# Hyena's transforms by residues of time modulo four, in a one-core encoder layer

## The reference

```python
h = rms_norm(x, norm_mix)
u_hy, q, k, v = split(h @ w_in, [1536, 2048, 2176])

def hyena_filter_spectra(...):                  # a sine network, 2 orders, forward and backward
    filt = (a @ w3).reshape(L, 2, 2, 512) * exp(-t * deltas)
    k2 = concatenate([fwd, 0, reversed bwd])    # 1024 rows of time
    return rfft(k2 / (sum(abs(k2), axis=0) + EPS), axis=0)

def hyena_mixer(u, short_w, short_b, skip, k_f):
    u = depthwise convolution of u over time, 3 taps, + short_b
    v, g1, g2 = split(u, 3)
    z = v
    for o, gate in enumerate((g1, g2)):
        z = gate * (irfft(rfft(z, n=1024) * k_f[o], n=1024)[:512] + skip[o] * z)
    return z

y = concat(group_rms_norm(y_hyena, 8 groups), group_rms_norm(y_attention, 8 heads))
x = x + y @ w_out
```

## Time and profile before

| what | value |
|---|---|
| runs, device us | 796.03, 793.9, 798.8; median 796.03 |
| span of the profiled execution | 791.7 us |
| instructions in it | 10886 |
| HBM read and written | 141.81 MB, 12.58 MB |
| mean DMA rate over the span | 195 GB/s |

### The profile page before, as it was taken

How to read it: one execution, slowest core, us unless ns; L and a number is a source line. 1 busy time by engine, 2 the same in 40 slices (tenths; PEclk the granted TensorE clock), 3 DMA queues, 4 the chain that set the end, 5 groups by cost and what they waited for, 6 DMA issues and landing times.

```text
span 791.7 us, 10886 instructions
## 1 busy us (share of the span) xinstructions
PE 747.9 (94%) x3680; PEld 607.8 (77%) x3680; DVE 603.7 (76%) x930; ACT 461.6 (58%) x689; POOL 78.0 (10%) x94
## 2 busy tenths in 40 slices
PE   5899999999999898889999999999999999999994
PEld 3664858788898787678787787888888888888882
DVE  5767482997799877835548568899899999999882
ACT  5952333131233988621559333787888888887782
POOL 0000000000000000000000001122222232222111
PEclk9999999999999999999999998999999999999997
DMA  8830203020120200022130675999999999999741
GB/s 291 298 107 1 84 23 106 27 80 1 38 96 27 78 31 1 2 62 97 54 116 18 246 294 182 420 364 385 379 372 383 373 391 372 369 369 383 306 159 21
DMA packets 28542, 146.53 MB, mean 185 GB/s; under 512 B 4791, under 2 KB 6711, under 8 KB 21976
## 3 DMA queue, kind: packets, MB, share of 16 engines
q1 hardware_dynamic: 23320, 135.53, 45.3%
q0 software_dynamic: 5184, 10.50, 5.0%
HBM read 141.81 MB, written 12.58 MB: 195 GB/s over the span
## 4 chain that ended last, share of the span: by engine, by line
PE 72%; DVE 15%; ACT 6%; DMA 4%; issue 3%; SPq 0%; POOL 0%; DVEq 0%; ACTq 0%; POOLq 0%
PE bank L1992 17%; PE bank L2378 11%; PE bank L2380 10%; PE bank L2379 10%; PE bank L1930 9%; PE bank L1937 3%; DMA slot<-in_w_down 2%; PE bank L2373 2%; PE bank L2004 1%; ACT w_hi L727 1%; PE bank L2292 1%; PE bank L2290 1%; PE bank L2291 1%; DVE w_lo L1165 1%; PE bank L2415 1%
## 5 line engine op out<-in xcount | busy, mean ns | idle before, releaser
L1849 DVE TENSOR_TENSOR e_lo<-slot,e_hi 128x1024 fp32r<-128x1024 f32 x192 | 221.4, 1218 | 9.4 <-ACT e_hi L1045 9.3
L1045 ACT ACTIVATE e_hi<-slot 128x1024 fp32r<-128x1024 f32 x192 | 188.2, 1061 | 7.7 <-DMA slot<-in_w_down 4.9
L1165 DVE TENSOR_TENSOR w_lo<-w_raw,w_hi 128x1024 fp32r<-128x1024 f32 x41 | 49.4, 1222 | 69.8 <-ACT w_hi L727 69.6
L727 ACT ACTIVATE w_hi<-w_raw 128x1024 fp32r<-128x1024 f32 x41 | 42.7, 1057 | 96.9 <-DMA w_raw<-in_w_in 63.2
L2378 PE MATMUL bank<-e_hi,hgT_hi 128*128 128x512 f32 x240 | 95.0, 396 | 0.3 <-DVE hgT_lo L1861 0.3
L2380 PE MATMUL bank<-e_hi,hgT_lo 128*128 128x512 f32 x240 | 93.6, 390 | 0.0
L2379 PE MATMUL bank<-e_lo,hgT_hi 128*128 128x512 f32 x240 | 93.4, 389 | 0.0
L2378 PEld LDWEIGHTS bank<-e_hi,hgT_hi 128*128 128x128 f32 x240 | 45.2, 189 | 9.5 <-DVE hgT_lo L1861 0.7
L2380 PEld LDWEIGHTS bank<-e_hi,hgT_lo 128*128 128x128 f32 x240 | 45.1, 188 | 9.6
L2379 PEld LDWEIGHTS bank<-e_lo,hgT_hi 128*128 128x128 f32 x240 | 45.1, 188 | 8.9
L2378 PE MATMUL bank<-e_hi,gaT_hi 128*128 128x512 f32 x120 | 48.1, 401 | 0.0
(11 more groups left out here) (395 smaller groups left out, 1671.6 us busy)
## 6 DMA issues: line engine op xcount, KB each, us to landing
slot<-in_w_down SPq DMA_DIRECT2D x16, 2048.0 KB, 16.6
slot<-in_w_gate SPq DMA_DIRECT2D x16, 2048.0 KB, 14.6
slot<-in_w_up SPq DMA_DIRECT2D x16, 2048.0 KB, 16.0
w_raw<-in_w_in SPq DMA_DIRECT2D x18, 512.0 KB, 3.5
w_raw<-in_w_out SPq DMA_DIRECT2D x8, 512.0 KB, 3.7
w_raw<-in_w_k_mem SPq DMA_DIRECT2D x4, 512.0 KB, 6.1
x_in<-in_x SPq DMA_DIRECT2D x4, 512.0 KB, 9.2
w_raw<-in_w_v_mem SPq DMA_DIRECT2D x4, 512.0 KB, 6.0
```

The lines of the kernel that those rows point to most:

```text
L727: act.activation(w_hi[ring(m)][:], w_raw[ring(m)][:], ACT.Copy).then_inc(s_wh, 1)
L1045: act.activation(e_hi[buffer(b, j)][:], slot[slot_][:, 1024 * part:1024 * (part + 1)], ACT.Copy).then_inc(s_ehi, 1)
L1165: dve.tensor_tensor(w_lo[slot_][:], w_raw[slot_][:], w_hi[slot_][:].bitcast(F32), ALU.subtract)\
L1849: dve.tensor_tensor(e_lo[slot_][:, at_], slot[slot_][:, at_], e_hi[buffer(b, j)][:].bitcast(F32), ALU.subtract)\
```

## The change

The convolutions are split by the residue r of time modulo four (`NR`) and the channels into two halves h of 256 (`HC`), where before it was parity and halves of the frequencies.

- **Forward and spectra.** A job is one residue, its cosine part in the left half of a bank and its sine part in the right: six fp32r products of 256 columns for z, fp32 products of 256 columns for the filter. DVE puts the residues together in two levels (`butterfly`, `second_sums`; `spec_sums` for the filter, whose residues 1 and 3 PE sums itself with a negated copy `dft_neg`).
- **Products.** `spectrum` and `filtered` take the place of `pointwise`: instructions of 2048 and 1024 elements.
- **Inverse and gates.** `inv_jobs` has `idft` as the stationary operand, so the results have time on partitions and need no transposes. The gates are turned instead (`gate_jobs`, copied out by ACT's `gate_rows`), and `gated` multiplies inverse and gate. `z_half_hi` and `z_half_lo` split order 1's input.
- **Norm and skip.** `gate_taps` puts the filter's norm into the gate's taps and bias; `skip_added` adds skip x norm to the filter's first row, for which `l1_row` sums the norm as a row. `skip_row` is a new load of 1024 values of 4 bytes.
- **Banks.** Jobs of this stage have fixed banks (`STAGE_BANKS`); filters use four.
- **Order.** g1, q, kv, g2 are the weights' order; forward, inverse and gates stand between single pieces of them; the constant products of this stage go. `roped` has the gains multiplied into its tables once (`rope_gains`) and ACT squares the keys. `outer_taps` takes two instructions of 511 for each block, not four of 255 or 256.
- **In the attention** the norm's sums are DVE reductions over the free axis; the rows of Hyena are multiplied by the inverse, turned (`hyena_rows`), and split as they leave PSUM (`hyena_rows_hi` on ACT, `hyena_rows_lo` on DVE).

```diff
+STAGE_BANKS = {"filt": lambda o, t, way: (2 * t + way) % 4, "mv": lambda j: 4 + j, "l1row": lambda o: 7, "l1": lambda o: 6 + o,
+               "spec": lambda o, h, r: 4 + SPEC_ORDER.index(r), "fwd": lambda o, h, r: 4 + R_ORDER.index(r),
+               "u": lambda c: c % 4, "q": lambda i: i, "kv": lambda i: i, "zT": lambda r: r,
+               "gT": lambda o, r: 6 + r % 2, "inv": lambda o, h, rp: 4 + 2 * h + rp, "kT": lambda j: 6 + j, "qT": lambda h: 6 + h}
...
+            c0 = COLS["skip"]
+            sp_.dma_start(skip_row[:].rearrange("o a (c p) -> o (a c) p", p=P),
+                          a["cols"][:, c0:c0 + 2 * CT].rearrange("p (o n) -> o n p", o=1),
+                          allow_slow_non_contiguous=True).then_inc(ld["skip"], 16)
             sp_.dma_start(rows[:], a["rows"]).then_inc(ld["rows"], 16)
...
-            weight_hi(4, 3)
-            abs_pair(0, 0)
-            abs_pair(0, 1)
-            weight_hi(7, 1)
-            abs_pair(0, 2)
-            abs_pair(0, 3)
+            weight_hi(4, 4)
+            for t in range(4):
+                abs_pair(0, t)
...
+            def skip_added(o):
+                job = ("l1row", o)
+                wait_filled(dve, job)
...
+                free(dve.scalar_tensor_tensor(skip_add[:], bank(job)[0:1, :], EPS, skip_row[:, o, :], ALU.add, ALU.mult), job)
+                first = sum_diff[o][0:1, 0, 0, :]
+                dve.tensor_tensor(first, first, skip_add[:], ALU.add).then_inc(s_skip, 1)
...
-            l1_add(0, 0)
-            l1_add(0, 1)
+            for t in range(4):
+                l1_add(0, t)
             weight_lo(8, 3)
-            l1_add(0, 2)
-            l1_add(0, 3)
+            skip_added(0)
             spec_sums(0, 0)
...
+            def spectrum(o, h):
+                x, k_, low = second_level, spec[:, o, h], inv_in[h]
+                link(butterfly(("fwd", o, h), x))
...
+                same = dve.tensor_tensor(products, x[:], k_, ALU.mult)
+                dve.tensor_tensor(low[:, 0:4], x[:, 0:4], k_[:, 4:8], ALU.mult)
+                link(dve.tensor_tensor(low[:, 4:8], x[:, 4:8], k_[:, 0:4], ALU.mult))
...
+            made = spectrum(0, 0)
+            weight_lo(15, 1)
+            filtered(0, 0, made)
+            weight_lo(16, 1)
+            made = spectrum(0, 1)
+            outer_taps(4)
+            weight_lo(17, 1)
+            filtered(0, 1, made)
+            gated(0, 0)
+            weight_lo(18, 1)
+            z_half_lo(0)
+            gated(0, 1)
+            memory_key_sums()
+            z_half_lo(1)
+            rope_gains()
+            made = spectrum(1, 0)
+            weight_lo(19, 2)
+            filtered(1, 0, made)
...
+            roped(0)
+            weight_lo(21, 1)
+            made = spectrum(1, 1)
+            weight_lo(22, 1)
+            filtered(1, 1, made)
+            roped(1)
+            weight_lo(23, 1)
+            key_sums()
+            roped(2)
+            roped(3)
+            weight_lo(24, 2)
...
+            main_chunk("v", slice(0, 2))
+            l1_row(1)
+            spec_jobs(1, 0)
+            main_chunk("v", slice(2, 3))
+            spec_jobs(1, 1)
+            main_chunk("v", slice(3, 4))
...
+            z_jobs()
...
+            fwd_jobs(0, 0)
+            main_chunk("g1", slice(0, 1))
+            fwd_jobs(0, 1)
+            main_chunk("g1", slice(1, 4))
+            inv_jobs(0, 0)
+            main_chunk("q", slice(0, 1))
+            gate_jobs(0)
+            main_chunk("q", slice(1, 2))
+            inv_jobs(0, 1)
+            fwd_jobs(1, 0)
+            main_chunk("q", slice(2, 3))
+            fwd_jobs(1, 1)
+            main_chunk("q", slice(3, 4))
+            main_chunk("kv")
+            main_chunk("g2")
+            inv_jobs(1, 0)
...
+            gate_jobs(1)
+            inv_jobs(1, 1)
```

More of the change, by code:

```diff
@@ L21 @@
 HALF = T // 2
+NR = 4
+RM = T // NR
+HC = CH // 2
+R_ORDER = (3, 1, 2, 0)
+SPEC_ORDER = (2, 0, 1, 3)
 NQ, NKV, HD = 8, 2, 64
@@ L1246, in spec_sums @@
[L1246 to L1261 removed]
+                c0 = COLS["short_w"]
@@ new lines, in gate_taps, with pair, halves, swapped_difference @@
+                taps = cols[:, c0:c0 + 48].rearrange("p (k c) -> p k c", c=12)[:, :, 4 * (o + 1):4 * (o + 2)]
+                link(dve.tensor_tensor(taps, taps, small[:, at_].unsqueeze(1).to_broadcast([P, 4, CT]), ALU.mult))
+            def pair(blocks, first, step):
+                return blocks[:, first:first + step + 1:step, :]
+            def halves(ap):
+                return ap.rearrange("p (w n) -> p w n", w=2)
+            def swapped_difference(dst, x, y):
+                for w in range(2):
+                    ins = dve.tensor_tensor(dst[:, (1 - w) * HC:(2 - w) * HC], x[:, w], y[:, w], ALU.subtract)
+                return ins
@@ new lines, in spec_sums @@
+            def spec_sums(o, h):
+                dst, sums, turned = spec[:, o, h], ("spec", o, h, 1), ("spec", o, h, 3)
+                even_sums(("spec", o, h))
+                a_, b_ = (halves(first_level[:, n, :]) for n in range(2))
+                wait_filled(dve, sums)
+                c_ = halves(bank(sums)[:])
+                dve.tensor_tensor(pair(dst, 0, 4), a_, c_, ALU.add)
+                free(dve.tensor_tensor(pair(dst, 2, 4), a_, c_, ALU.subtract), sums)
+                wait_filled(dve, turned)
+                d_ = halves(bank(turned)[:])
+                dve.tensor_tensor(pair(dst, 1, 6), b_, d_, ALU.add)
+                free(dve.tensor_tensor(pair(dst, 3, 2), b_, d_, ALU.subtract), turned)
+                wait_freed(dve, turned)
@@ L1273, in _ @@
             filters(1, 1)
-            l1_add(1, 0)
             spec_sums(0, 1)
             filters(1, 2)
-            l1_add(1, 1)
-            weight_lo(11, 1)
-            filters(1, 3)
-            l1_add(1, 2)
-            l1_add(1, 3)
-            weight_lo(12, 2)
+            filters(1, 3)
+            for t in range(4):
+                l1_add(1, t)
+            dve.wait_ge(ld["rows"], 16)
+            dve.wait_ge(ld["rope"], 16)
+            dve.wait_ge(s_gq, 1)
+            skip_added(1)
@@ L1454, in _ @@
             dve.tensor_reduce(small[:, 240:272], q_sq[:].rearrange("p i (h d) -> p (i h) d", d=HD), AX.X, ALU.add).then_inc(s_ms, 1)
-            for c in range(CT):
-                skipped(1, c)
+            outer_taps(8)
+            gated(1, 0)
+            gated(1, 1)
             dve.wait_ge(s_hrms, 3)
             dve.reciprocal(small[:, 240:272], small[:, 240:272]).then_inc(s_qinv, 1)
-            def hyena_inverse():
-                dve.wait_ge(s_hroot, 1)
-                dve.reciprocal(small[:, 280:312], small[:, 280:312]).then_inc(s_hrec, 1)
```

722 lines of the change are left out of this document (373 added, 349 removed).

## The result

The changed kernel takes 812.37 us (median of 4 runs, 811.08 to 815.21), the kernel before beside it 797.41 (4 runs). The ratio on record is 1.0212, with a 95% interval of 1.0173 to 1.0252 (the two medians divide to 1.0188, which lies in it): slower by about 2%, and outside the range of 786 to 809. The profiled execution's span grew from 791.7 to 809.2, by 17.5 us; 1.6 were forecast.

A forecast was written before the change was run, and what follows sets the result against it. PE bounded the Hyena stage before; DVE was to bound its second stretch after the change. Span 791.7 + 5.1 - 3.5 (attention) = 793.3; with runs' median 4.3 above the span, 797.6 us, range 786 to 809.

The forecast's parts named there:

- the first stretch: From the first filter product to DVE's first `spectrum`, which was forecast to start at 129.2 us.
- the waits and the tail of the second: First `spectrum` to first score maximum: 1.6 us of DVE waiting before piece 24's split, at 236.6; score maximum at 264.0, +5.1.
- the attention: From the first score maximum on: 3.5 us less, as sums by products and part of the norm go.
- DVE becomes the bound: From first `spectrum` to first score maximum: DVE's queued work sums to 124.7 us, against 111.9 before; PE's savings become waits.
- Step (a): Filter products have four banks, not eight; the fifth waits for DVE's first `filters` at 41.67, PE leaves them 2.8 us later.
- (b): In the first stretch the memory values' 48 products end at 57.2 us, where they ended at 54.4 before.
- the 3 us that the forecast has for the clock: Slow clock behind PE's long waits at two places before the first `spectrum`: 1.7 us each, 3 taken in all.
- D: Rival, the clock: PE comes back slow from four more waits in the second stretch, 7 us more, 805; chance 0.15.
- E: Rival, the row of skips: its small packets hold SP's queue and shift what follows by 8.5 us, 806; chance 0.11.
- A: The prediction's own case: DVE bounds the second stretch, attention gains 3.5 us; 790 to 804, chance 0.47.
- B: Rival, attention gains in full: about -10 us instead of -3.5, so 791, or 788 without the slow clock; chance 0.20.

The follow-up runs named there:

- e11: Changed kernel, second stretch reordered: DVE splits pieces 19 to 25 a step earlier, gates and last inverse ahead of the keys, which get own banks; ratio 1.0093.
- e2: Changed kernel with six waits of PE filled by constant products whose result nobody reads; ratio 1.0160.
- e7: Changed kernel with the transposes of Hyena's rows writing PSUM at steps of four, so that the copies have no step; ratio 1.0222.
- e5: Changed kernel with the load of the row of skips issued behind weight piece 6; ratio 1.0216.
- e9: Changed kernel with two absolute values ahead of weight piece 7 again, and skip_added ahead of weight splits 8 to 10; ratio 1.0123.
- e6: Changed kernel with the lo parts of weight pieces 19 to 25 made on POOL, not DVE; ratio 1.0161.
- e1: Changed kernel with the load of the row of skips issued behind weight piece 5; ratio 1.0250.

## Why the prediction was wrong, point by point

The mechanism that it named, DVE's longer sum and PE's waits behind it, is what the trace shows. Its sum failed in three terms: the first stretch (4.2 us), the waits and the tail of the second (5.9), and the attention (6.5).

**DVE becomes the bound: the sum was right, and it did not set the time.** The sum was 124.7 us, the trace has 122.39 busy. But DVE idled 18 of the 140.7 us, and e11 took 10.5 of them away with the same sum. PE's waits came where they were put: 6.2 at piece 19 (7 forecast), 4.1 and 2.4 at 22 and 23 (5 each), 3.9 for the outer taps (3.5), 2.3 at `l1_row` (2.2), 3.4 for `skip_added` (3.8).

**The first stretch, 4.2 us late.** Step (a) failed: the first `filters` came 1.9 later than 41.67, which is what the row of skips costs (about 2 us, above) and the prediction had put at nothing; and the four filter products behind PE's 4.3 us of waiting ran at 0.50 for the most part, 5.4 us for four, where the same four take 3.7 in e2 at 1.00. The prediction counted the 2.8 us of delay there and not the clock behind it. Everything from (b) on moved with it: v started at 86.9, not 81.6 (the 3 us that the forecast has for the clock are added behind v).

**The second stretch, 5.9 us longer.** DVE waited 5.2 us, not 1.6, before the split of piece 24 (for ACT's split of piece 15, for order 0's inverse, for q), and the tail behind it took 30.0, not 27.4: the constant products 1.7 of that. These are 6.2; DVE's own work ahead of the tail was some 0.3 shorter.

**Attention: the step with the wrong sign.** It forecast 3.5 less from rows that stood on the chain before; 3.0 more were measured. Work taken off that chain gave nothing up to the eleventh exponential; that ACT's exponentials, a chain next to it, are why, is argued and not shown. And the steps at which work is issued were read as neutral: the root's two table loads cost 3.1 us where they were moved to, with or without a weight split beside them, PE lost its clock behind them, and at the seventeenth exponential, where before has paid for its own root, 2.1 of the 3.0 are there already. Behind that the stepped copies, 0.5 us longer each on ACT and not priced at all, took what the change gave: without them (e7) 2.6 of the 3.0 are back.

**The rivals.** D and E were each priced to decide alone and put aside at 0.15 and 0.11; both came in part, on top of A, not in its place. E's 8.5 us were about 2. Of D the slow places came, but its 7 us in the second stretch no run shows; what was measured is the clock's price in the first, 4.5 for 3. B had the attention's gain; in sum there is none.

**What stays open.** Whether a slow place comes at all differs between executions (e5 had it at 268, the changed kernel's profile did not), and single stations spread by up to 2.6 us between kernels with the same first stretch. No run filled PE's waits for pieces 19 and 22, so the clock's share in the second stretch is not known. The split of e9's 6.0 us into waits and clock was not tried.

## What to carry to other kernels

A change that moves work from the engine that bounds to one that has room must be laid out again: nearly the same work cost 812 us in the order given and 792 in another, with PE's waits filled. When the engine that was always busy begins to wait, price the clock behind each wait, not the wait alone, and keep it busy with products that cost nothing else. And price a work item that is only moved to another step anew at that step: the root's two table loads cost 3.1 us at each of the three that were tried.

## What the runs showed of the hardware

- POOL beside DVE: a DVE instruction with both inputs in SBUF that met a POOL subtraction waited for its end (a sum of 512 elements took 2.77 us, not 0.69), those with an input in PSUM did not, and work that POOL took over for 8.2 us of DVE's time cost DVE 11.9 elsewhere. POOL seems to wait as well, as far as its spans, which are rough, tell: one subtraction that began beside such a DVE instruction took 4.10 us, not 2.40, and ended 2.25 behind it (226.91 in e6).
- A load of 1024 values of 4 bytes made the next issue on its queue take 3.54 us, and held up the weight piece in flight beside it (piece 6 in e1, issued at 36.00, split at 41.24 after a wait).
- A transpose that writes PSUM at steps of four costs what one without steps does (16 records with a mean of 273 ns in both kernels), while an ACT copy that writes SBUF at such steps took 1.21 us and not 0.70.
